# Modulation units in pairs that share a PSUM bank, and at other places of the unit order

## What is computed

```python
# first block
h = rmsnorm(x, norm_mix_g); p = h @ w_in
x = x + concat([sliding_window_attention(...), sigmoid(mo) * mlstm(...)]) @ w_out
x = x + cross_attention(rmsnorm(x, norm_xattn_g), rmsnorm(mem, norm_mem_g), wq_x, wkv_x, wo_x)
u = rmsnorm(x, norm_ffn_g) @ w_up
x = x + (silu(causal_conv(u[:, :2816])) * u[:, 2816:]) @ w_down
x = rmsnorm(x, norm_final_g)
# second block; c_act = silu(c) is one vector of 1024
for layer in (0, 1):
    shift, scale, gate = split(c_act @ w_ada[layer] + b_ada[layer], 3)     # the modulation
    h = rms(x) * norm_g[layer] * (1 + scale) + shift
    if layer == 0:
        y = gated_delta_mixer(h, w_in_a, ...) @ w_out_a
    else:
        s, t = split(c_act @ w_ada_kv + b_ada_kv, 2)                       # the modulation of k and v
        kv = (rms(x) * kv_norm_g * (1 + t) + s) @ w_kv
        y = stick_breaking_attention(h @ w_in_b, kv) @ w_out_b
    x = x + gate * y
```

## Time and profile before

| | |
|---|---|
| median of the runs | 980.85 us (980.75, 980.85, 982.5) |
| the profiled execution, its own time | 981.4 us |
| its span in the profile | 979.6 us |
| PE busy | 898.2 us, 92% of the span |
| DVE busy | 585.4 us, 60% |
| ACT busy | 503.6 us, 51% |
| DMA queue q1 | 146.94 MB, 41.2% of 16 engines' time |
| TensorE's granted clock, mean | 0.953 (1 is 2.4 GHz, 0.5 is 1.2 GHz) |

### The profile page before, as it was taken

The page is one execution under the profiler, slowest core; times in us unless marked ns, Lnnn a source line. Parts: engine busy times, 40 slices in busy tenths (PEclk is TensorE's granted clock), DMA queues, the critical chain, the costliest instruction groups (busy, mean ns, idle before and its releaser), DMA issues.

```text
span 979.6 us, 18062 instructions
## 1 busy us (share of the span) xinstructions
PE 898.2 (92%) x7660; PEld 818.4 (84%) x7660; DVE 585.4 (60%) x1225; ACT 503.6 (51%) x1029; POOL 0.5 (0%) x5
## 2 busy tenths in 40 slices
PE   3978899999999999999969899989897979999998
PEld 3967698998898999999968787869796878988888
DVE  5378656566666777776556666665545466533345
ACT  5345554344445555555455636262645457456762
POOL 0000000000000000000000000000000000000000
PEclk9899899999999999999996999999999779999999
DMA  9322444573256666655661432323222134642211
GB/s 345 139 81 105 154 173 152 193 257 131 86 178 253 228 227 236 257 196 192 201 228 58 158 130 92 125 86 130 87 87 87 46 133 153 250 156 82 71 60 43
DMA packets 22544, 148.09 MB, mean 151 GB/s; under 512 B 2624, under 2 KB 3136, under 8 KB 6336
## 3 DMA queue, kind: packets, MB, share of 16 engines
q1 hardware_dynamic: 22464, 146.94, 41.2%
HBM read 145.88 MB, written 1.05 MB: 150 GB/s over the span
## 4 chain that ended last, share of the span: by engine, by line
PE 78%; DVE 12%; ACT 7%; issue 1%; DMA 1%; SPq 0%; DVEq 0%; ACTq 0%
PE ps L1864 56%; PE ps L1877 3%; DVE wlo L1385 2%; PE ps L2086 1%; PE ps L1885 1%; PE ps L1907 1%; DVE kT L1382 1%; ACT L1003 1%; PE ps L2096 1%; PE ps L2176 1%; DVE vt L1382 1%; ACT tmp L1077 1%; PE ps L2109 1%; PE ps L2068 1%; PE ps L2167 1%
## 5 line engine op out<-in xcount | busy, mean ns | idle before, releaser
L1864 PE MATMUL ps<-p0hi,whi 128*128 128x256 f32 x1128 | 340.4, 302 | 16.8 <-DVE p0lo L1385 12.5
L1864 PE MATMUL ps<-p0lo,whi 128*128 128x256 f32 x1128 | 325.2, 288 | 0.0
L1864 PE MATMUL ps<-p0hi,wlo 128*128 128x256 f32 x1128 | 324.8, 288 | 0.0
L1385 DVE TENSOR_TENSOR wlo<-raw,whi 128x512 fp32r<-128x512 f32 (+2 forms) x436 | 273.0, 660 | 20.6 <-ACT whi L1023 19.1
L1864 PEld LDWEIGHTS ps<-p0hi,whi 128*128 128x128 f32 x1128 | 222.3, 197 | 36.2 <-issue 24.8
L1023 ACT ACTIVATE whi<-raw 128x512 fp32r<-128x512 f32 (+2 forms) x436 | 239.7, 599 | 9.2 <-DMA raw<-wst 7.8
L1864 PEld LDWEIGHTS ps<-p0lo,whi 128*128 128x128 f32 x1128 | 222.9, 198 | 1.0 <-issue 0.8
L1864 PEld LDWEIGHTS ps<-p0hi,wlo 128*128 128x128 f32 x1128 | 222.3, 197 | 0.0
L1864 PE MATMUL ps<-zhi,whi 128*128 128x256 f32 x176 | 49.3, 280 | 0.0
L1864 PE MATMUL ps<-zlo,whi 128*128 128x256 f32 x176 | 49.1, 279 | 0.0
L1864 PE MATMUL ps<-zhi,wlo 128*128 128x256 f32 x176 | 49.1, 279 | 0.0
(11 more groups left out here) (344 smaller groups left out, 1517.0 us busy)
## 6 DMA issues: line engine op xcount, KB each, us to landing
raw<-wst SPq DMA_DIRECT2D x125, 1024.0 KB, 4.8
raw<-wsd SPq DMA_DIRECT2D x16, 704.0 KB, 4.7
x<-xT SPq DMA_DIRECT2D x4, 256.0 KB, 5.0
m_x<-memT SPq DMA_DIRECT2D x1, 1024.0 KB, 17.5
outT<-x SPq DMA_DIRECT2D x4, 256.0 KB, 2.1
cst<-con SPq DMA_DIRECT2D x1, 544.0 KB, 12.6
smo<-conr SPq DMA_DIRECT2D x1, 192.0 KB, 11.7
vc<-vec SPq DMA_DIRECT2D x1, 187.5 KB, 2.4
```

The source lines that it names most:

```text
L1385: return v.tensor_tensor(lo, src, hi.bitcast(F32), ALU.subtract)
L1864: ins = t.matmul(o, a, b, start=first and q == 0, stop=last and q == len(ops) - 1, skip_group_check=True)
```

## The change

Four things, in the order of the diff. The modulation units are taken in pairs by a new function `two_ada`, and stand at other places of the order: pairs ahead of `mqk` 0 and 2, `mv` 0, `mo` 0, `xk` 0 and 2, `xq` 0, `xo` 2; none in `up`; two pairs between `down` and `qkva` 0; pairs ahead of `qkva` 1, 2 and 3, `za` 2, `sbk` 0 and `sbv` 2. `adarow` of a pair streams both units into both halves of `stats`, one `adacp` copies 512 columns, one `adacol` has four matmuls and one `adaadd` four columns. The rows of the two pairs between `down` and `qkva`, and of the one between `outa` and `sbk`, are emitted by hand amid the norm's jobs. The sum of norm kv goes to ps3 instead of `stats`.

```diff
     ada = [("ada0", i) for i in range(12)] + [("adakv", i) for i in range(8)] + [("ada1", i) for i in range(12)]
 
-    def mixed(name, first, n, every):
-        for i in range(first, first + n):
-            add(name, i)
-            if every and i % every == every - 1:
-                add(*ada.pop(0))
+    def two_ada():
+        add(*ada.pop(0))
+        add(*ada.pop(0))
 
     add("aq", 0, 2)
     add("akv", 0)
-    mixed("mqk", 0, 4, 2)
-    mixed("mv", 0, 2, 2)
-    add("mo", 0, 2)
-    mixed("xk", 0, 4, 2)
+    two_ada()
+    for name, n in (("mqk", 4), ("mv", 2), ("mo", 2)):
+        for i in range(0, n, 2):
+            add(name, i, 2)
+            two_ada()
+    add("xk", 0, 2)
+    two_ada()
+    add("xk", 2, 2)
     add("xv", 0)
-    mixed("wout", 0, 4, 2)
+    add("wout", 0, 4)
     add("xv", 1, 2)
+    two_ada()
     add("xq", 0, 4)
     add("xv", 3)
-    mixed("xo", 0, 4, 2)
-    mixed("up", 0, 22, 2)
+    add("xo", 0, 2)
+    two_ada()
+    add("xo", 2, 2)
+    add("up", 0, 22)
     add("down", 0, 16, 11, 128)
+    two_ada()
+    two_ada()
     for i in range(4):
         for part in range(3):
             add("qkva", 4 * part + i)
-            if part != 1:
-                add(*ada.pop(0))
-    add("za", 0, 4)
+        if i < 3:
+            two_ada()
+    add("za", 0, 2)
+    two_ada()
+    add("za", 2, 2)
     add("outa", 0, 4)
+    two_ada()
     add("sbk", 0, 4)
-    mixed("sbv", 0, 4, 1)
+    add("sbv", 0, 2)
+    two_ada()
+    add("sbv", 2, 2)
...
     def ada_part(self):
         k = self.carried.pop(0)
         self.run_late(True)
+        self.ada_rows(k)
+        self.add("adacp", k)
+        self.late.append([3, k])
+
+    def ada_rows(self, k):
         self.add("adarow", k)
-        self.add("adacp", k)
-        self.loaded_free.add(k)
+        self.loaded_free.update((k, k + 1))
         self.load_units()
-        self.late.append([3, k])
...
         if is_ada(self.units[k]):
             self.carried.append(k)
-            self.prep = max(self.prep, k + 1)
-            self.unit += 1
+            self.prep = max(self.prep, k + 2)
+            self.unit += 2
...
         self.flush_lows()
+        self.run_late(True)
+        first, second = self.carried
+        self.carried = []
+        self.ada_rows(first)
         add("f_ones")
+        add("adacp", first)
         add("f_sum")
         add("f_r12")
+        add("adacol", first)
+        add("adaadd", *self.units[first][:2])
+        self.ada_rows(second)
         add("f_rs")
         add("f_m", "a")
         for _ in self.mod_steps("a"):
             pass
+        add("adacp", second)
+        self.late.append([3, second])
         add("fin")
...
         self.run_to(self.at("sbk"))
+        self.run_late(True)
+        kv_pair, = self.carried
+        self.carried = []
+        self.ada_rows(kv_pair)
         self.rstd("kv")
         add("f_m", "kv")
         for _ in self.mod_steps("kv"):
             pass
+        add("adacp", kv_pair)
+        self.late.append([3, kv_pair])
...
         stats = ps[7]
+
+        def sum_bank(site):
+            return ps[3][:, 0:T] if site == "kv" else stats[:, 0:T]
+
...
                 elif kind == "adacp":
                     k, = i
                     e.wait_ge(*on("adarow", k))
-                    act.activation(arow[:, :], stats[:, T:2 * T], ACT.Copy).then_inc(*tick("adacp"))
+                    act.activation(arow[:, :], stats, ACT.Copy).then_inc(*tick("adacp"))
...
-                    v.tensor_tensor(mod[:, col + 2 * n:col + 2 * n + 2], stats[:, T:T + 2], V(bname, 2 * n, 2), ALU.add).then_inc(*tick("adaadd"))
+                    v.tensor_tensor(mod[:, col + 2 * n:col + 2 * n + 4], stats[:, 0:4], V(bname, 2 * n, 4), ALU.add).then_inc(*tick("adaadd"))
...
-                    r = raw[k % NRAW]
-                    e.wait_ge(*arrived(k))
                     e.wait_ge(*on("csilu", "c"))
                     stats_free()
                     stat.append(("adacp", k))
-                    for c in range(KC):
-                        g = 32 * (c % 4)
-                        ins = t.matmul(stats[g:g + 32, T:2 * T], cact[:, c, :], r[:, c * T:(c + 1) * T], start=c < 4, stop=c >= 4)
+                    for u in range(2):
+                        r = raw[(k + u) % NRAW]
+                        e.wait_ge(*arrived(k + u))
+                        for c in range(KC):
+                            g = 32 * (c % 4)
+                            ins = t.matmul(stats[g:g + 32, u * T:(u + 1) * T], cact[:, c, :], r[:, c * T:(c + 1) * T], start=c < 4, stop=c >= 4)
                     ins.then_inc(*tick("adarow"))
                 elif kind == "adacol":
                     k, = i
                     e.wait_ge(*on("adacp", k))
                     stats_free()
                     stat.append(("adaadd", *units[k][:2]))
-                    for m in range(2):
-                        ins = t.matmul(stats[:, T + m:T + m + 1], arow[:, m * P:(m + 1) * P], ones[:, 0:1], start=True, stop=True)
+                    for m in range(4):
+                        ins = t.matmul(stats[:, m:m + 1], arow[:, m * P:(m + 1) * P], ones[:, 0:1], start=True, stop=True)
                     ins.then_inc(*tick("adacol"))
```

More of the change, by code:

```diff
@@ L802, in at, with ada_pair @@
             return plan.at(name, i)
+        def ada_pair(k):
+            return k if ("adarow", k) in rank else k - 1
         def unit_done(name, i):
@@ L828, in program @@
         acc = sb("acc", [P, T])
-        arow = sb("arow", [P, T])
+        arow = sb("arow", [P, 2 * T])
         ph = ExitStack()
@@ L982, in _ @@
                     if is_ada(units[k - NRAW]):
-                        e.wait_ge(*on("adarow", k - NRAW))
+                        e.wait_ge(*on("adarow", ada_pair(k - NRAW)))
                     else:
@@ L1054, in _ @@
                     lnexp()
-                    own.mark(act.activation(rs[:, :], stats[:, 0:T], ACT.Ln, bias=C("biases", 0, 1), scale=1.0 / D))
+                    own.mark(act.activation(rs[:, :], sum_bank(site), ACT.Ln, bias=C("biases", 0, 1), scale=1.0 / D))
                     e.wait_ge(*own.last)
@@ L1499, in _ @@
                     if name == "outa":
-                        e.wait_ge(*on("adaadd", "ada0", 11))
+                        e.wait_ge(*on("adaadd", "ada0", 10))
                         for m in range(2):
@@ L1510, in _ @@
                     e.wait_ge(*unit_done("outb", n))
-                    e.wait_ge(*on("adaadd", "ada1", 11))
+                    e.wait_ge(*on("adaadd", "ada1", 10))
                     for m in range(2):
@@ L1553, in _ @@
                     site, = i
-                    col, gain, last = {"a": (8, "g_a", ("ada0", 7)), "kv": (56, "g_kv", ("adakv", 7)), "b": (32, "g_b", ("ada1", 7))}[site]
+                    col, gain, last = {"a": (8, "g_a", ("ada0", 6)), "kv": (56, "g_kv", ("adakv", 6)), "b": (32, "g_b", ("ada1", 6))}[site]
                     e.wait_ge(*on("adaadd", *last))
@@ L1890, in _ @@
                     e.wait_ge(*landed("con"))
-                    stats_free()
-                    stat.append(("rs", site))
-                    t.matmul(stats[:, 0:T], ones, acc[:, :], start=True, stop=True).then_inc(*tick("ones"))
+                    if site != "kv":
+                        stats_free()
+                        stat.append(("rs", site))
+                    t.matmul(sum_bank(site), ones, acc[:, :], start=True, stop=True).then_inc(*tick("ones"))
                 elif kind == "f_ones":
```

## The result

The changed kernel takes 988.12 us (median of 20 runs, 979.23 to 990.11), the kernel before 981.4 (median of 20, 975.25 to 984.26). The ratio is 1.0052, 95% interval 1.0034 to 1.007: slower. I had forecast 974.7 with a range of 968.5 to 981.0. The runs of the changed kernel lie in two groups: 14 of the 20 at 987.6 to 990.1 with a mean granted clock of 0.934 to 0.937, 6 at 979.2 to 980.4 with 0.945 to 0.947. (The expectation of again says 13 and 7.) The six lie inside my range, but even they are about 5 us above the forecast. The profiled execution (989.19 us, span 987.4) is one of the first group; that of before was 981.4, span 979.6. Among the experiments one run of prep_mixsingle, 1245 us at a granted clock of 0.644, is left out.

The account below looks back on a forecast made before the run. TensorE was taken to bound the kernel, with 78% of the chain. Terms -18.3 + 3.4 + 2.9 + 0.5 + 0.8 + 0.8 + 7.8 - 1.2 - 2.8 = -6.1 us took 980.85 to 974.7, range 968.5 to 981.0.

Parts of the forecast that it names:

- `qkva` and `za`: Mixer stage: eight single modulation units become four pairs, with as many chain waits as before: -1.2 us.
- The slower rival: Pairs' narrow columns let the clock fall, slowing the part behind each of twelve pairs: +16.5, 991.3 us; chance 0.10.
- The late weights: `down` to `qkva`: weights of `qkva` 0 wait behind `fin`, part 0 and gate matmuls at half clock: +7.8 us (3.0 to 9.1).
- The two rivals on them: `qkva` 0 weights: late but cheap as part 0 restores the clock (970.0, chance 0.15); not late at all (966.9, 0.06).
- Up: Up projection: eleven modulation units leave at 1.63 us each, plus one unit's columns; VectorE keeps up: -18.3 us.
- The `mqk`, `xq` and front terms: Ahead of `up`: dense pairs for singles +3.4, `mqk` 0 +2.9, `mqk` 2 +0.5, `xq` 0 +0.8 us.
- The quarter of the way that I took for `mqk` 0: Pair at `mqk` 0: a quarter between bounds 2.0 and 5.3 us, for time at half clock: +2.9.
- `outa` to `sbq`: Stage after the mixer: `sbk` pair's rows fit a wait, columns +0.8, one pair +3.0, four singles -6.5: -2.8 us.
- my three signs of being wrong: Part 0 follows norm a as before; up falls to VectorE's pace; clock drops behind pairs at `mv`, `xk` or `xo`.
- The filled waits: Pairs' rows placed in TensorE's waits were taken as free or nearly so; the rival, not free: 979.9 us, chance 0.14.

Follow-up runs that it names:

- again: The changed kernel rerun with nothing edited, for a second profile and the spread of its runs: 982.54 us, ratio 1.0033.
- prep_mixsingle: Changed kernel with the weights of `qkva` 0 prepared in the boundary and single modulation units in `qkva` and `za`: 971.36 us, ratio 0.9888.
- fill_ctl: Changed kernel plus 72 matmuls of constants, 18 each ahead of `d_x` of level 3 where TensorE is dense, not in the waits: 990.0 us, ratio 1.0074.
- b_mixpair: Kernel before with only the eight modulation units of `qkva` and `za` put in four pairs: 980.81 us, ratio 1.001.
- mixsingle: Changed kernel with the eight modulation units of `qkva` and `za` single at their earlier places: 977.31 us, ratio 0.9966.
- fill: Changed kernel plus 18 matmuls of constants, result unread, in each of the four waits for `d_rs`: 969.47 us, ratio 0.9886.
- prep_fill2: Changed kernel, `qkva` 0 weights prepared in the boundary, constants in the `d_rs` waits, ahead of second gate matmuls, in norm kv, ahead of last `d_v1`: 957.46 us.
- prep_fill: Changed kernel with `qkva` 0 weights prepared in the boundary and 18 matmuls of constants in each of the four `d_rs` waits: 961.55 us, ratio 0.9799.
- prep: Changed kernel with the weights of `qkva` 0 prepared in the boundary, lo pieces ahead of norm a: 969.02 us, ratio 0.9883.

## Why the prediction was wrong

**The failed step** is "*`qkva` and `za`.* Eight singles become four pairs: 11.9 - 13.0 = -1.2. Chain waits are as many as before." The stage was to get 1.2 us shorter and got 10.6 longer. The price of the pairs was right (-1.2 with the waits filled, in stages of 223.1 and 224.3 us), and the four waits for `d_rs` are as long as before (2.33 us and three of 1.96). Wrong was that I took the clock of a stage as fixed: 0.50 was granted for 58.7 us of it and not for 34.0. The mixer stage in 19 profiles of this study (fill_ctl, which has more work in it, left out; us, h as above; six of them here):

| kernel | length | h |
|---|---|---|
| before | 231.9 | 34.0 |
| after | 242.5 | 58.7 |
| b_mixpair | 233.6 | 34.8 |
| mixsingle | 230.3 | 30.7 |
| fill | 223.1 | 13.7 |
| prep_fill2 | 222.7 | 10.2 |

A line through the 19 is 217.7 + 0.42 h, none further from it than 1.2 us. From before to after h grew by 24.7: 10.4 of the 10.6 us. The Trainium skill ("TensorE: Matmul & The Clock Gate", section "HAM oscillation — how this bites in real kernels") prices throttled time at 1 - 1.2/2.4, 0.5 us lost for each; the runs give 0.42, a little less. That TensorE also waits in such stretches may be why; no run here tests it.

**The slower rival** had the sign and not the mechanism. It blamed the narrow columns of pairs; yet at `mv`, `mo` and `xk`, where pairs stand in dense work, the clock stayed at 0.99 to 1.00, and b_mixpair ran its pairs at 1.00. The clock falls behind the waits for `d_rs`, in the kernel before too: behind the first it is at 0.50 for 6.8 us there and for 13.7 in the changed kernel, behind the second for 3.4 and 17.1. That the loss hangs on these waits is shown by filling them. What decides how long the clock stays low is not: with one and the same program the changed kernel took 979.2 or 990.1. That pairs raise the odds is shown by counts alone (20 of 32 runs, 1 of 12 in b_mixpair, none of 12 in mixsingle), and whether the late weights do it through the longer low stretch ahead or through the phase stays open. In that sense the rival was half right: the pairs are part of the cause, not by their columns alone.

**The late weights** went as forecast: behind `fin`, part 0 at half clock, part 1 28.3 us behind the end of `down` (I had said some 28), 7.9 us by prep_fill against 7.8. That this fits so well is in part luck: up to `qkva` 4 preparing them gives 9.5 us with the waits filled and 10.7 without, and of the 9.5 some is lost again later (the mixer stage of prep_fill is 224.4 us, that of fill 223.1). The two rivals on them fall: neither did part 0 bring the clock back, nor was it hidden. They also cost through the stage behind (prep: 13 to 19 us below the changed kernel's two medians of 988 and 982).

**The sizes.** Up gave 17.1 of 18.3: a unit is 5.76 us as forecast, but 3.4 us at its start are at 0.50, where none was before. VectorE keeps its pace: line 1559 at 340.38, 346.14 and 351.90, 5.76 apart, as long as a unit on TensorE. The `mqk`, `xq` and front terms were 1.1 too high together, although 3.4 us more are at 0.50 there. (The quarter of the way that I took for `mqk` 0 gives 2.8, not 2.9.) `outa` to `sbq` gave 1.3 more than forecast, but 7.6 us less are at 0.50 there, which is worth some 3 by the slope above (an estimate). So my -2.8 was too large by itself, and the clock hid it. The 2.1 us behind `sbq` 0, where I had no term, are stretches at 0.50 around 877 and 959 that before did not have.

**The signs.** None of my three signs of being wrong came: part 0 came late, the up stretch is bound by TensorE, and the clock stood at 0.99 and more behind the pairs at `mv`, `xk` and `xo`. They watched every stage but the one that failed.

**The filled waits** were nearly free, as forecast; the pair at `xq` 0 left a wait of 0.26, the one at `sbk` 0.68:

```profile
227.51 0.36 PE L1903 MATMUL ps<-p0hi,whi 128*128 128x256 f32 x1 [0.26 <-issue]
...
802.71 0.70 PE L1934 MATMUL ps<-acc,cst 128*128 128x256 f32 x2 [0.68 <-DVE acc L1452]
```

## What to carry to other kernels

Cost a stage at both of TensorE's clocks, and look in the profile for what stands at 0.50 behind a wait (of 1.96 and 2.33 us here): there the wait costs its own length and, by the slope above, 0.42 of the time at 0.50 that follows. A change can lose by lengthening that time with every wait as long as before. Where such a wait can't be removed, matmuls of constants that just fit into it are worth trying (the changed kernel went from 0.5% behind the kernel before to 1.1% ahead of it, and the kernel before itself gained 0.9%), and real work of the right length is better only if it doesn't open a wait elsewhere. Moving work across a stage boundary also moves the preparation of the next weights: keep it ahead of the norm and of any long VectorE step.

## What the hardware showed that I had not expected

One program on one chip gave 979.4 and 989.1 us, and the mean granted clock told the two apart in every run (0.945 and more, 0.941 and less). A wait of 2.33 us between matmuls was followed by 13.5 us at 1.2 GHz with TensorE busy for all 13.5, and behind a wait of 12.56 us it was busy for 18.70 us at 1.2 GHz. Seven matmuls of 1.86 us in all, placed ahead of a part, gave the gate matmuls 3.77 us where they otherwise took 6.64.
